# Decode attention over 640 instead of 1024 cached positions per sample in a hybrid decoder step

## The chip, the cores and the metric

The kernel runs on one core of one Trainium2 chip. The metric is the device time of one execution in microseconds. The core has TensorE (PE; its weight loads are listed as PEld), VectorE (DVE), ScalarE (ACT), GpSimd (POOL) and SyncE (SP), which issues most of the transfers; 16 DMA engines carry them.

## The reference

One inference step of one decoder layer: a prompt of 256 tokens and 8 samples of 4 new tokens (32 rows), 288 tokens together, all in fp32, with model width 1024. The normalized rows are projected by `w_in`, the attention and the state-space branch are joined and projected by `w_out`, and a mixture of 32 experts (top 4) follows. The part that the change touches is the attention of the samples, with 8 heads of 64 and a cache of 1024 past positions:

```python
DILATED_PATTERNS = ((128, 1), (512, 4), (2048, 16))

def dilated_attn_decode(q, k_all, v_all, slopes):
    T = q.shape[1]                      # 4
    M = k_all.shape[1] - T              # 1024
    for window, dil in DILATED_PATTERNS:
        steps = jnp.arange(window // dil + 1)
        idx = M + jnp.arange(T)[:, None] - dil * steps[None, :]
        valid = idx >= 0
        kg, vg = k_all[:, jnp.maximum(idx, 0)], v_all[:, jnp.maximum(idx, 0)]
        s = jnp.einsum('bthe,btkhe->bthk', q, kg) * scale
        bias = -slopes[:, None] * (dil * steps).astype(jnp.float32)[None, :]
        s = jnp.where(valid[:, None, :], s + bias, -jnp.inf)
        lse = jax.nn.logsumexp(s, axis=-1)
        outs.append(jnp.einsum('bthk,btkhe->bthe', jnp.exp(s - lse[..., None]), vg))
        lses.append(lse)
    return merge_by_denominator(outs, lses)
```

Past position p is reached by new token t if it lies within 128 of it, within 512 at a distance that is a multiple of 4, or at any distance that is a multiple of 16. So all positions from 512 on can be reached by one token or another (with t from 0 to 3, every residue of 4 occurs), and of the first 512 only those whose number is 0, 1, 2 or 3 modulo 16: 512 + 128 = 640.

## The kernel before

The kernel is one program with an order written out by hand for each engine. `mixer_steps()` returns the list `STEPS` that TensorE, VectorE and ScalarE all walk, each doing its own part of a step. The step `proj` is one of 32 projections of 128 output columns (8 matmuls of 288 columns each). Between the projections stand the steps of the samples' attention, of the prompt's attention (`p_score`, `p_trans`, `p_out`), of the convolution (`conv`, `silu`, `conv_out`), of dt (`dt`, `dt_sum`) and the turns of results back to token rows (`nat`).

The samples' attention computes all three patterns at once. Every position gets one bias, minus slope times distance plus the logarithm of the number of patterns that reach it, and -1e30 where none does; one softmax over all of them then gives the merged result. For each sample b there is a block of steps around two projections:
- `ktr`: VectorE turns the keys into columns, in four block transposes (32 by 32 blocks) of 128 by 1024 (L1231 to L1240), out of two ring slots into `kTb`, 16 times 288 columns: 256 columns of old positions (four positions side by side in the 128 lanes) and 32 new ones.
- `kscore`: TensorE makes 16 matmuls of 288 columns against the zero-padded queries `Qz` in four groups of 32 output partitions (L1827); VectorE adds the bias, keeps the maximum and writes `Pb` (L1263, L1264).
- `max_out`, `max_back`, `exp`, once for four samples: the maxima cross over TensorE (L1831, L1834), and ScalarE takes the exponentials (L904).
- `ptrans`: TensorE transposes the probabilities, two times 128 columns and once 32 (L1841, L1842), and ScalarE copies them back in another order (L909, L911).
- `pv`: 16 steps, 8 for each four samples; each is a tile of 128 positions of `cache_win_v` for four samples, 4 matmuls of 512 columns into bank 3 (L1859). `pv_new` adds the new rows (L1866), `gather_o` (L1870) puts the heads together.

Cached keys, cached values and `w_in` come through a ring of five 1 MB slots (`MIX_RING = 5`). `ring_items()` writes out the order: for each sample two halves of its keys and a pair of `w_in` tiles, then four times a pair of `w_in` tiles and four value tiles. SP issues them in this order (L574); the load of item n first waits until item n - 5 has been used (`mix_used`), and everything behind it in the queue waits too:

```python
            if kind == "w_in":
                eng.wait_ge(sem("w_used"), i // 2 + 1)
            elif kind == "k":
                eng.wait_ge(sem("k_used"), 2 * i + ITEMS[n][2] + 1)
            else:
                eng.wait_ge(sem("v_used"), i + 1)
```

After the mixer's steps come the scan of the states, the output projection (L2086), the router, and the experts (L2296, L2320), whose 192 weight units of 2 MB SP loads at L593. The last tile of `w_out` is loaded after a wait on `M_ready` (L577), and the first expert unit stands behind it in the queue.

Of the kernel before, what the change touches and what calls it, by code (L numbers as in the profile page):

```python
# [16 lines left out]
P = 128  # L17
# [7 lines left out]
PAST = 1024  # L25
# [43 lines left out]

XP = 3 + SEQ + DB * (3 + DT)  # L70
# [4 lines left out]
def shape_constants():  # L75
# [51 lines left out]
    put("bias_new", new.reshape(P, -1))  # L127
    consts = np.concatenate(parts, 1)
    col = np.arange(2 * P)
    d_old = PAST + t_row[:, None] - (2 * P * row_q[:, None] + 8 * (col % 32)[None, :] + (col // 32)[None, :])  # L130
    bias_old = bias(h_row[:, None], d_old).astype(np.float32)
# [8 lines left out]
def mixer_steps():  # L140
# [51 lines left out]
    steps.extend(("pv", t) for t in range(4))  # L192
# [6 lines left out]
    steps.extend(("pv", t) for t in range(4, 8))  # L199
# [9 lines left out]
    steps.extend(("pv", t) for t in range(8, 12))  # L209
# [7 lines left out]
    steps.extend(("pv", t) for t in range(12, 16))  # L217
# [33 lines left out]
ITEM_AT = {item: n for n, item in enumerate(ITEMS)}  # L251


def hymba_step(nc, a, o):

    ctx = ExitStack()
    with ctx:
# [34 lines left out]

        ident = const("ident")
# [51 lines left out]
        kTb = d3(work_take(16 * 288), 288)  # L345
# [4 lines left out]
        bias_o = work_take(2 * P)  # L350
        r_Pb = work_take(DB * 288)
        Pb = d3(r_Pb, 288)
# [21 lines left out]
        Xs = d3(const("bias_new"), P)  # L374
# [66 lines left out]
        def mix_used(eng, n):  # L441
# [4 lines left out]
            elif kind == "k":  # L446
                eng.wait_ge(sem("k_used"), 2 * i + ITEMS[n][2] + 1)
            else:
                eng.wait_ge(sem("v_used"), i + 1)
# [5 lines left out]
        def mix_full(eng, item):  # L455

            eng.wait_ge(sem(f"slot_full{mix_slot(item)}"), 16 * (ITEM_AT[item] // MIX_RING + 1))

        MIX_LOADS = [len([item for item in ITEMS if mix_slot(item) == s]) for s in range(RING)]
# [75 lines left out]
        def _(sp):  # L535
# [4 lines left out]
            w_out = a["w_out"][0].rearrange("(k p) c -> p k c", p=P)  # L540
            for n, item in enumerate(ITEMS):
# [7 lines left out]
                if item == ("v", 12):  # L549
# [17 lines left out]
                elif item[0] == "w_out":  # L567
                    dst, src = d3(slot(s), D), w_out[:, 2 * item[1]:2 * item[1] + 2, :]
                elif item[0] == "k":
                    dst, src = slot(s), a["cache_win_k"][0, item[1]].rearrange("(p k) h e -> p (k h e)", k=8)[:, SLOT * item[2]:SLOT * item[2] + SLOT]  # L570
                else:
                    grp, t = item[1] // 8, item[1] % 8
                    dst, src = d3(slot(s), AW), a["cache_win_v"][0, 4 * grp:4 * grp + 4, t * P:t * P + P].rearrange("b p h e -> p b (h e)")
# [197 lines left out]
        def _(act):  # L771
# [98 lines left out]
            for kind, i in STEPS:  # L870
# [34 lines left out]
                elif kind == "ptrans":  # L905
                    act.wait_ge(sem("ptrans_ps"), i + 1)
                    bank = 6 + i % 2
                    for half in range(2):
                        nc.scalar.activation(Pb[:, i, P * half:P * half + P].rearrange("p (q j c) -> p j q c", q=4, j=4),  # L909
                                             ps[:, bank, P * half:P * half + P].rearrange("p (j q c) -> p j q c", j=4, q=4), ACT.Copy)  # L910
                    nc.scalar.activation(d3(Pb[0:NS, i, 2 * P:2 * P + 32], 8), d3(ps[0:NS, bank, 2 * P:3 * P], 32)[:, :, 0:8], ACT.Copy).then_inc(sem("PT_ready"), 1)  # L911
# [212 lines left out]
        def _(dve):  # L1124
# [73 lines left out]
            for kind, i in STEPS:  # L1198
# [27 lines left out]
                elif kind == "krep":  # L1226
                    dve.wait_ge(sem("rep_ps"), 2)
                    nc.vector.tensor_copy(kTb[:, :, 2 * P:2 * P + NS].rearrange("p (j m) c -> p m j c", j=4),
                                          ps[:, 4, :].rearrange("p (m j c) -> p m j c", m=4, j=4)).then_inc(sem("krep_ready"), 1)
                elif kind == "ktr":  # L1230
# [3 lines left out]
                    for half in range(2):  # L1234
                        mix_full(dve, ("k", i, half))
                        rows = slot(mix_slot(("k", i, half))).rearrange("p (k m c) -> p k m c", k=4, m=16)
# [1194 lines left out]
```

## Time and profile before

| | us |
|---|---|
| median of 3 runs | 1264.44 (1264.29 to 1267.62) |
| span of the profiled execution | 1263.9 |
| TensorE busy | 1223.5 (97%) |
| VectorE busy | 373.5 (30%) |
| ScalarE busy | 241.7 (19%) |
| GpSimd busy | 49.2 (4%) |
| HBM read | 468.47 MB, 376 GB/s over the span |

An engine's busy time is the union of its instructions' times; TensorE's matmuls overlap, so that a busy TensorE need not be at its peak. An fp32 matmul is recorded as two instructions, and its duration includes its way through the array: the time that a row of them takes is read from the starts of its first and of the row that follows. In a timeline a line is a run of like instructions: start, length, engine, line of the kernel, operation, output and input, shape, count, and in brackets the idle time before it and what ended it. Of a shape like "128*32 128x288" the first part is rows by columns of the stationary operand, the second the moving one.

### The profile page before, as it was taken

How to read it: one execution, taken by the hardware profiler on the slowest of the kernel's cores; microseconds unless marked ns; L12 is line 12 of the kernel's file. 1: busy time of each engine (PE TensorE's matmuls, PEld its weight loads, DVE VectorE, ACT ScalarE, POOL GpSimd, SP SyncE). 2: the span in 40 equal slices, each digit the busy share in tenths (PEclk: the TensorE clock that was granted, in tenths of full speed). 3: DMA queues.
4: the chain of work that ended last, by engine and by line, in shares of the span. 5: the costliest groups of instructions: out<-in, count | busy, mean ns of one | idle time of the engine just before them, and what ended most of it. 6: DMA issues, size and time to landing. Idle time of an engine off the chain costs nothing.

```text
span 1263.9 us, 14652 instructions
## 1 busy us (share of the span) xinstructions
PE 1223.5 (97%) x5750; PEld 520.6 (41%) x5750; DVE 373.5 (30%) x756; ACT 241.7 (19%) x492; POOL 49.2 (4%) x46
## 2 busy tenths in 40 slices
PE   9999999999999999999999999999999999999997
PEld 6766666544433333333333333333333333333332
DVE  2468532775330321213031221213030312212122
ACT  2014343544201111120111111020111111111103
POOL 0000031503000000000000000000000000000000
PEclk9999999999999999999999999999999999999999
DMA  9697679249799999999999999999999999999996
GB/s 284 232 319 264 245 268 352 90 143 347 299 428 413 429 426 429 429 427 430 428 428 428 429 428 429 428 429 428 428 429 428 427 430 427 428 429 427 427 428 252
DMA packets 67439, 476.21 MB, mean 377 GB/s; under 512 B 7704, under 2 KB 25396, under 8 KB 40428
## 3 DMA queue, kind: packets, MB, share of 16 engines
q1 hardware_dynamic: 65278, 471.87, 91.0%
q10 hardware_dynamic: 1582, 2.03, 0.5%
q0 software_dynamic: 544, 1.84, 0.4%
q8 instruction: 23, 0.38, 0.1%
q14 instruction: 12, 0.10, 0.0%
HBM read 468.47 MB, written 7.24 MB: 376 GB/s over the span
## 4 chain that ended last, share of the span: by engine, by line
PE 75%; DMA 21%; DVE 2%; ACT 2%; issue 1%; SPq 0%; ACTq 0%; DVEq 0%
PE ps L2296 28%; DMA ring<-in_w 20%; PE ps L2320 11%; PE ps L1784 10%; PE ps L2234 4%; PE ps L2086 4%; PE ps L2226 2%; PE ps L2218 2%; PE ps L1827 1%; PE ps L2220 1%; PE ps L2284 1%; PE ps L2009 1%; PE ps L2304 1%; PE ps L1803 1%; PE ps L1859 1%
## 5 line engine op out<-in xcount | busy, mean ns | idle before, releaser
L2296 PE MATMUL ps<-ring,own 128*64 128x512 f32 x1536 | 340.1, 593 | 10.0 <-DMA ring<-in_w 10.0
L2296 PEld LDWEIGHTS ps<-ring,own 128*64 128x64 f32 x1536 | 111.7, 137 | 223.4 <-issue 194.3
L1658 DVE TENSOR_SCALAR own<-ps 128x512 f32<-128x512 f32 x32 | 22.1, 692 | 531.3 <-PE ps L2296 531.3
L2320 PE MATMUL ps<-ring,own 128*64 128x512 f32 x768 | 171.3, 594 | 4.7 <-ACT own L1055 4.6
L1784 PE MATMUL ps<-own,ring 128*128 128x288 f32 x512 | 131.6, 410 | 1.4 <-DVE own L1161 1.1
L2296 PE MATMUL ps<-own 128*64 128x512 f32 x512 | 115.9, 592 | 2.3 <-DMA own<-in_w 2.3
L1784 PEld LDWEIGHTS ps<-own,ring 128*128 128x128 f32 x512 | 95.7, 191 | 31.7 <-issue 3.3
L2320 PEld LDWEIGHTS ps<-ring,own 128*64 128x64 f32 x768 | 56.0, 137 | 111.3 <-issue 109.9
L2234 PE MATMUL ps<-own 128*128 128x512 f32 x180 | 88.5, 617 | 0.0
L1061 ACT ACTIVATE own<-ps 64x512 f32<-64x512 f32 x60 | 35.5, 592 | 206.5 <-PE ps L2320 205.8
L1649 DVE TENSOR_TENSOR own<-ps,own 128x512 f32<-128x512 f32 x34 | 21.9, 686 | 172.4 <-PE ps L2242 172.4
L2296 PEld LDWEIGHTS ps<-own 128*64 128x64 f32 x512 | 37.8, 136 | 68.3 <-issue 61.0
L2320 PE MATMUL ps<-own 128*64 128x512 f32 x256 | 58.5, 597 | 5.5 <-issue 4.1
L1050 ACT ACTIVATE own<-own 128x512 f32<-128x512 f32 x32 | 20.1, 627 | 217.2 <-DVE own L1658 217.2
L1055 ACT ACTIVATE own<-ps 128x512 f32<-128x512 f32 x32 | 19.1, 597 | 217.9 <-PE ps L2304 217.5
L2234 PEld LDWEIGHTS ps<-own 128*128 128x128 f32 x180 | 29.1, 187 | 48.5 <-issue 48.5
L2086 PE MATMUL ps<-ring,own 128*128 128x512 f32 x96 | 47.1, 612 | 0.0
L1239 DVE STREAM_TRANSPOSE ring<-ring 128x1024 f32<-128x1024 f32 x32 | 37.0, 1212 | 0.0
L2320 PEld LDWEIGHTS ps<-own 128*64 128x64 f32 x256 | 18.7, 135 | 39.3 <-issue 33.5
L2226 PE MATMUL ps<-own 128*128 128x512 f32 x64 | 31.8, 618 | 0.0
L2218 PE MATMUL ps<-own 128*128 128x512 f32 x64 | 31.8, 618 | 0.0
L2086 PEld LDWEIGHTS ps<-ring,own 128*128 128x128 f32 x96 | 16.3, 189 | 19.0 <-issue 18.8
(367 smaller groups left out, 978.3 us busy)
## 6 DMA issues: line engine op xcount, KB each, us to landing
ring<-in_w SPq DMA_DIRECT2D x143, 2048.0 KB, 29.7
own<-in_w SPq DMA_DIRECT2D x48, 2048.0 KB, 28.3
ring<-in_w_in SPq DMA_DIRECT2D x16, 1024.0 KB, 6.2
ring<-in_cache_win_k SPq DMA_DIRECT2D x16, 1024.0 KB, 6.6
ring<-in_cache_win_v SPq DMA_DIRECT2D x16, 1024.0 KB, 8.8
ring<-in_w_out SPq DMA_DIRECT2D x6, 1024.0 KB, 10.5
ring<-in_state_ssm SPq DMA_DIRECT2D x8, 512.0 KB, 10.3
out_ssm_sample<-ring SPq DMA_DIRECT2D x8, 512.0 KB, 9.6
```

The costliest lines, as they stand in the source:

```text
L1050: nc.scalar.activation(sg, xg, ACT.Sigmoid, scale=ALPHA).then_inc(sem("sig_ready"), 1)
L1061: nc.scalar.activation(ysb[C * u:C * u + C, 512 * half:512 * half + 512], ps[C * half:C * half + C, 4, :], ACT.Copy).then_inc(sem("ysb_rea ...
L1239: last = nc.vector.transpose(to[:, k:k + 2], rows[:, k:k + 2])
L1649: nc.vector.tensor_tensor(xT[:, 4 * half:4 * half + 4, :], d3(ps[:, 3 + 2 * half, :], 2 * C), vecs[:, 28 + 4 * half:32 + 4 * half].unsquee ...
L1658: nc.vector.tensor_scalar(xg_o, hid[:, 0], LIMIT, None, ALU.min).then_inc(sem("glu_ready"), 1)
L1784: last = nc.tensor.matmul(ps[:, i % 2, 0:TOK], w[:, k, (i % 2) * P:(i % 2) * P + P], xnT[:, k, :], start=(k == 0), stop=(k == KT - 1))
L2086: last = nc.tensor.matmul(ps[:, h_bank(c, half), :], mixT[:, k, cols(c)], w_rows(k)[:, 512 * half:512 * half + 512], start=(i == 0), stop= ...
L2218: nc.tensor.matmul(ps[:, 6 + half, :], GT[:, cols(0)], ysb[:, 512 * half:512 * half + 512], start=True, stop=True)
L2226: last = nc.tensor.matmul(ps[:, 3 + half, :], GT[:, cols(1)], ysb[:, 512 * half:512 * half + 512], start=True, stop=True)
L2234: last = nc.tensor.matmul(ps[:, 6 + half, :], S1[0:n, c, :], xn[0:n, c, 512 * half:512 * half + 512], start=(c == 0), stop=(c == 2))
L2296: last = nc.tensor.matmul(ps[C * half:C * half + C, 1 + m, :], xT[:, k, C * u:C * u + C], rows[:, D * half + 512 * m:D * half + 512 * m + ...
L2320: last = nc.tensor.matmul(ps[C * half:C * half + C, 4, :], gT[:, (k % 4) * P + C * (k // 4):(k % 4) * P + C * (k // 4) + C], rows[:, 512 * ...
```

## The change

Of each sample's 1024 old positions only 640 are loaded: the last 512 (from `LATE`) whole, and of the first 512 those whose number is 0 to 3 modulo 16, as 32 groups of 4 rows.
- Keys: one ring slot a sample instead of two (512 rows, two block transposes of 128 by 1024), and 128 early rows in one of two own buffers, `k_early`, with one transpose of 128 by 512. `kTb` and `Pb` have 192 columns instead of 288 (128 late, 32 early, 32 new). Before it loads the early rows of sample b (from 2 on), SP waits until both transposes of sample b - 2 are done.
- Values: 5 tiles instead of 8 for each four samples, the fifth made of early rows in four loads of 256 KB. The 10 `pv` steps stand where the 16 stood, 3, 2, 3 and 2 instead of 4 in each place, and the ring's order follows.
- `ptrans`: one full transpose, then for the 32 early columns four matmuls with picked columns of the identity, each into its own 32 partitions, then the transpose of the new columns. ScalarE copies 128, 32 and 32 columns instead of 128, 128 and 32.
- The bias of new rows and early rows comes with `bias_old` (640 columns, it was 256) and no longer with the constants (256 columns fewer). `Xs` gets its own place.

```diff
-            items += [("k", b, 0), ("k", b, 1), ("w_in", 8 + 2 * b)]
-    for i in range(4):
-        items += [("w_in", 24 + 2 * i)] + [("v", 4 * i + t) for t in range(4)]
+        items += [("k", b), ("w_in", 8 + 2 * b)]
+    for i, tiles in enumerate((range(3), range(3, 5), range(5, 8), range(8, 10))):
+        items += [("w_in", 24 + 2 * i)] + [("v", t) for t in tiles]
...
+            def early_rows(cache, sample):
+                return a[cache][0, sample, 0:LATE].rearrange("(g s) h e -> g s (h e)", s=STRIDE)[:, 0:DT]
...
-                if item == ("v", 12):
+                if item == ("v", 8):
                     sp.wait_ge(sem("conv_o"), 3)
...
+                elif is_early(item):
+                    for b in range(4):
+                        sp.dma_start(slot(s)[:, AW * b:AW * b + AW], early_rows("cache_win_v", 4 * (item[1] // TILES_V) + b)).then_inc(sem(f"slot_full{s}"), 16)
+                    continue
                 elif item[0] == "k":
-                    dst, src = slot(s), a["cache_win_k"][0, item[1]].rearrange("(p k) h e -> p (k h e)", k=8)[:, SLOT * item[2]:SLOT * item[2] + SLOT]
+                    b = item[1]
+                    if b >= 2:
+                        sp.wait_ge(sem("k_used"), 2 * b - 2)
+                    sp.dma_start(k_early[b % 2], early_rows("cache_win_k", b)).then_inc(sem(f"slot_full{s}"), 16)
+                    dst, src = slot(s), a["cache_win_k"][0, b, LATE:PAST].rearrange("(p k) h e -> p (k h e)", k=4)
...
+                    nc.vector.transpose(kTb[:, :, P:OLD], d3(k_early[i % 2], 32)).then_inc(sem("k_used"), 1)
...
-                            last = nc.tensor.matmul(ps[32 * j:32 * j + 32, 4 + i % 2, 0:288], Qz[:, 4 * j + m, i, :], kTb[:, 4 * j + m, :], start=(m == 0), stop=(m == 3))
+                            last = nc.tensor.matmul(ps[32 * j:32 * j + 32, 4 + i % 2, 0:OLD + NS], Qz[:, 4 * j + m, i, :], kTb[:, 4 * j + m, :], start=(m == 0), stop=(m == 3))
...
-                    for half in range(2):
-                        nc.tensor.transpose(ps[:, bank, P * half:P * half + P], Pb[:, i, P * half:P * half + P], ident)
-                    nc.tensor.transpose(ps[0:NS, bank, 2 * P:3 * P], Pb[:, i, 2 * P:2 * P + NS], ident).then_inc(sem("ptrans_ps"), 1)
+                    nc.tensor.transpose(ps[:, bank, 0:P], Pb[:, i, 0:P], ident)
+                    for q in range(4):
+                        own_rows = ident.rearrange("p (j q c) -> p q j c", j=4, q=4)[:, q]
+                        nc.tensor.matmul(ps[32 * q:32 * q + 32, bank, P:OLD], Pb[:, i, P:OLD], own_rows, start=True, stop=True)
+                    nc.tensor.transpose(ps[0:NS, bank, 2 * P:3 * P], Pb[:, i, OLD:OLD + NS], ident).then_inc(sem("ptrans_ps"), 1)
...
-                        w = d3(Pb[:, 4 * grp + b, P * (t % 2):P * (t % 2) + P], 32)[:, t // 2]
+                        w = d3(Pb[:, 4 * grp + b, 0:OLD], 32)[:, t]
```

## Rows read from the trace of the kernel before

**Rows 1.** Stretches: busy time of PE, PEld, DVE, ACT, POOL; clock, DMA share, GB/s
```profile
0.00:217.00 217.00, 210.26 (x1258) 144.54 (x1258) 105.42 (x274) 61.34 (x196) 18.00 (x23) 0.99 0.81 278
400.00:1200.00 800.00, 779.52 (x3396) 279.04 (x3394) 162.75 (x266) 105.12 (x167) 0.00 (x0) 1.00 1.01 428
```

**Rows 2.** The SP queue from 245 us: its longest wait; its timeline there
```profile
SPq L577 <- DVE own L1368: 48.4, 1, 48.4
...
265.71 0.42 SPq L593 DMA_DIRECT2D ring<-in_w  x1
```

**Rows 3.** TensorE's timeline around the scores of samples 1 and 2
```profile
69.51 2.15 PE L1827 MATMUL ps<-ring,own 128*32 128x288 f32 x32
71.58 4.16 PE L1784 MATMUL ps<-own,ring 128*128 128x288 f32 x16
...
80.22 2.15 PE L1827 MATMUL ps<-ring,own 128*32 128x288 f32 x32
```

**Rows 4.** TensorE's timeline around value tiles, and late in the stage
```profile
153.72 0.62 PE L1892 MATMUL ps<-own 128*59 128x128 f32 x4 [1.38 <-ACT ring L926]
...
166.34 3.62 PE L1859 MATMUL ps<-ring 128*32 128x512 f32 x32
169.89 0.78 PE L1884 MATMUL ps<-own 128*128 128x16 f32 x6
...
209.93 1.04 PE L1870 MATMUL ps<-ring,own 128*32 128x512 f32 x2
...
212.13 0.55 PE L1911 MATMUL ps<-own,ring 128*128 128x128 f32 x3
```

**Rows 5.** ScalarE's timeline from 161 to 167 us
```profile
161.38 0.40 ACT L930 ACTIVATE ring<-ring,own 128x128 f32<-128x128 f32 x1
...
161.78 0.49 ACT L931 ACTIVATE ring<-ring,own 128x256 f32<-128x256 f32 x1
...
166.53 0.41 ACT L915 ACTIVATE own<-ps 128x288 f32<-128x288 f32 x1 [0.71 <-PE ps L1878]
```

**Rows 6.** VectorE at sample 4 (key transposes, convolution, maxima); TensorE there
```profile
93.28 4.62 DVE L1239 STREAM_TRANSPOSE ring<-ring 128x1024 f32<-128x1024 f32 x4
...
101.97 0.27 DVE L1271 TENSOR_REDUCE own<-ps 4x32 f32<-4x128 f32 x1
...
92.36 4.16 PE L1784 MATMUL ps<-own,ring 128*128 128x288 f32 x16
...
102.55 0.22 PE L1834 MATMUL ps<-own 4*128 4x4 f32 x1 [1.36 <-DVE own L1272]
```

**Rows 7.** TensorE: transposes, the sum matmuls, four narrow records in one column group
```profile
108.78 0.49 PE L1803 MATMUL ps<-own 128*128 128x128 f32 x3
109.10 0.38 PE L1841 MATMUL ps<-own,ring 128*128 128x128 f32 x2
...
125.03 0.49 PE L1803 MATMUL ps<-own 128*128 128x128 f32 x3
125.45 0.24 PE L1846 MATMUL ps<-own 128*32 128x1 f32 x8
125.53 2.13 PE L1827 MATMUL ps<-ring,own 128*32 128x288 f32 x32
...
215.18 0.31 PE L1741 MATMUL ps<-own 128*32 128x32 f32 x4
215.42 0.23 PE L1748 MATMUL ps<-own 32*32 32x16 f32 x2
```

**Rows 8.** The wait of projection 30 on TensorE, and its load's issue on SP
```profile
190.69 4.16 PE L1784 MATMUL ps<-own,ring 128*128 128x288 f32 x16 [0.28 <-DMA ring<-in_w_in]
...
184.74 0.37 SPq L574 DMA_DIRECT2D ring<-in_w_in  x1
```

**Rows 9.** DMA issues from 60 to 138 us: count, size, median us to landing
```profile
ring<-in_cache_win_k SPq DMA_DIRECT2D x10, 1024.0 KB, 7.0
ring<-in_w_in SPq DMA_DIRECT2D x7, 1024.0 KB, 5.8
```

More of the change, by code:

```diff
@@ L126, in shape_constants @@
     new = np.where(own & (d_new >= 0), bias(h_row[:, None, None], d_new), NEG)
-    put("bias_new", new.reshape(P, -1))
     consts = np.concatenate(parts, 1)
-    col = np.arange(2 * P)
-    d_old = PAST + t_row[:, None] - (2 * P * row_q[:, None] + 8 * (col % 32)[None, :] + (col // 32)[None, :])
-    bias_old = bias(h_row[:, None], d_old).astype(np.float32)
+    col = np.arange(OLD)[None, :]
+    lane = 32 * row_q[:, None] + col % 32
+    place = np.where(col < P, LATE + 4 * lane + col // 32, STRIDE * (lane // 4) + lane % 4)
+    dropped = np.setdiff1d(np.arange(PAST), place)
+    assert place.size == np.unique(place).size * P // 4 and (bias(0, PAST + np.arange(DT)[:, None] - dropped) == NEG).all()
+    old = bias(h_row[:, None], PAST + t_row[:, None] - place)
+    tails = np.concatenate([np.broadcast_to(old[:, None, P:], new[:, :, 0:P // 4].shape), new], 2)
+    bias_old = np.concatenate([old[:, 0:P], tails.reshape(P, -1)], 1).astype(np.float32)
     d_prompt = r[:, None, None] + P - np.arange(2 * P)[None, None, :] + 0 * np.arange(AH)[None, :, None]
@@ L191, in mixer_steps @@
     steps.extend([("silu", 10), ("silu", 11), ("conv_out", 0)])
-    steps.extend(("pv", t) for t in range(4))
+    steps.extend(("pv", t) for t in range(3))
     steps.append(("conv_out", 1))
@@ L198, in mixer_steps @@
     steps.extend([("ptrans", 6), ("ptrans", 7), ("dt", 0), ("sums", 1)])
-    steps.extend(("pv", t) for t in range(4, 8))
+    steps.extend(("pv", t) for t in range(3, 5))
     steps.append(("dt_sum", 0))
@@ L208, in mixer_steps @@
     steps.extend([("p_out", 1), ("p_trans", 2), ("p_score", 3)])
-    steps.extend(("pv", t) for t in range(8, 12))
+    steps.extend(("pv", t) for t in range(5, 8))
     back(27)
@@ L216, in mixer_steps @@
     steps.extend([("p_out", 3), ("p_trans", 4), ("p_score", 5)])
-    steps.extend(("pv", t) for t in range(12, 16))
+    steps.extend(("pv", t) for t in range(8, 10))
     steps.append(("pv_new", 1))
@@ L455, in mix_full @@
         def mix_full(eng, item):
-            eng.wait_ge(sem(f"slot_full{mix_slot(item)}"), 16 * (ITEM_AT[item] // MIX_RING + 1))
-        MIX_LOADS = [len([item for item in ITEMS if mix_slot(item) == s]) for s in range(RING)]
+            before = [other for other in ITEMS[:ITEM_AT[item]] if mix_slot(other) == mix_slot(item)]
+            eng.wait_ge(sem(f"slot_full{mix_slot(item)}"), 16 * sum(loads_of(other) for other in before + [item]))
+        MIX_LOADS = [sum(loads_of(item) for item in ITEMS if mix_slot(item) == s) for s in range(RING)]
         def w_out_slot(i):
@@ L1865, in _ @@
                     for b in range(4):
[L1866 removed]
+                        last = nc.tensor.matmul(ps[32 * b:32 * b + 32, 3, :], Pb[0:NS, 4 * i + b, OLD:OLD + NS], v[0:NS, 2, :], start=False, stop=True)
                     last.then_inc(sem("pv_ps"), 1)
```

57 lines of the change are left out of this document (34 added, 23 removed).

## The prediction

> **What bounds the kernel now.** I read the table of stretches first [rows 1]. Up to 217 us (projections, attention, convolution) TensorE is busy for 210.3 us, and DMA has room (0.81 of its engines). Then the state scan and the output projection follow, to 340 us. From 400 us on the experts' weights arrive at 428 GB/s with the DMA share at 1.01. So the first stage is bound by TensorE's instructions in their written order, the last by the stream of weights. What is between them decides whether an early gain lasts: the queue of SP waits 48.4 us, in one piece, for VectorE's last decay product before it loads the last tile of w_out and, behind it, the first expert weights [rows 2]. Nothing of the stream is fetched ahead, so its start is tied to the end of the computation and moves one for one with it. I therefore add up what TensorE's path loses before 217 us and carry the sum to the end.
>
> An fp32 matmul stands in the trace as two records (the 32 projections of 8 matmuls are 512 records in the page), and columns count in it: the 16 score matmuls of one sample (32 records, 288 columns) take 2.07 us from their start to the start of the next work, the 16 value matmuls of four tiles (32 records, 512 columns) 3.55 us [rows 3, 4]. Per record that is 65 and 111 ns, ratio 1.71, against 1.78 in columns.
>
> **Scores.** Each sample's 16 matmuls go from 288 to 192 columns (128 + 32 old, 32 new). The two prices give (3.55 - 2.07) / 224 = 6.6 ns for each column of a set, with 0.17 us that stays. Then 96 columns fewer are 0.63 us, a set costs 1.44 us, and eight samples save **5.0 us**. All of it lies on the path: the next projection starts at the set's end [rows 3]. Bounds: 5.5 us if all of 2.07 us shrinks with the columns, nothing if the weight loads set the pace (a rival).
>
> **Values.** Ten tiles instead of sixteen, each 512 columns at 6.6 ns / 4 = 0.85 us to 3.55 / 4 = 0.89 us; at 0.87 six fewer are **5.2 us**. They go in four places (one, two, one, two tiles). In the last three the next waits are covered. After the second place the first thing needed is the evacuated dt product; ScalarE has it 0.60 us after the place where the tiles begin (166.94 against 166.34 us), and two tiles last 1.7 us [rows 4, 5]. After the third comes projection 30, whose weights I take below. After the last, a prompt score needs 2.2 us from its end to its transposes (209.93 to 212.13 us [rows 4]), against two tiles, 1.7, and the new rows' 1.0 us. In the first place it is not so. There TensorE already waits 1.38 us for ScalarE [rows 4], which first has to run four exponentials and two pairs of SiLU. Taking one tile away there lengthens the wait by 0.87 us. The exponentials shrink from 288 to 192 columns; the rows of 128 and 256 columns give 0.7 ns a column, 0.07 us each, 0.3 us for four [rows 5]. So **0.6 us** of the gain is given back.
>
> **VectorE's stall.** Each sample's keys cost four 32 by 32 block transposes of 1024 columns, 4.62 us; now two of 1024 and one of 512, 2.9 us (half of a long one, 0.6, for the short one; it is not in the trace, so 0.5 to 1.2). The biased copy of the scores shrinks too. From sample 3 on VectorE has 4.1 us of convolution behind them, and at sample 4 it is late: TensorE waits 1.36 us for the maxima [rows 6]. From the end of the previous scores (92.36 us) TensorE needs 8.8 us to the place of that wait (102.55 less 1.36). VectorE after the change needs 0.1 (start) + 0.6 (scores and maximum; 0.8 before, from 92.5 to 93.28 us) + 2.9 + 4.1 + 0.6 (maxima) = 8.3 us. The stall goes: **1.4 us** (1.1 if the short transpose costs as much as a long one). Next late is TensorE itself. The transposes of the other samples are covered, and their 14 us buy nothing.
>
> **Transposed probabilities.** Three transposes of a step take 0.32 us, 0.11 each (108.78 to 109.10 us [rows 7]). Of the three of a sample's probabilities one full one goes (0.11 us) and four matmuls of 32 columns come, each with its own 32 output partitions. The nearest rows are the four sum matmuls (weights 128 by 32, four column groups, one column): 0.08 us for 8 records. Before them the transposes of the step ahead, 0.32 us elsewhere, take 0.42 (125.03 to 125.45 us), so going over to narrow column groups costs 0.10 us; the 0.17 us left over in the score sets is the likely price of the way there and back [rows 3, 7]. Four small matmuls between two full transposes thus cost 0.08 + 0.05 for 31 more columns + 0.17 = 0.30 us, less 0.11: 0.19 us a sample, **+1.5 us** (bounds 0, if no switch is paid, and +4.5, if the records run one after the other at 60 ns as in one group, 215.18 to 215.42 us [rows 7]). I take 1.5 because it is made of rows with this very shape of weights. ScalarE's copies get no longer.
>
> The Trainium skill, "TensorEngine Tiling (Array Packing)", section "Instruction Overhead", says that a matmul has an overhead of about 60 cycles and that one with a free size of 1 takes as long as one of 60. Read as a floor for each record it would make the eight records 0.2 us instead of 0.13, an estimate from that page, and the sum 0.6 us smaller; the eight records in 0.08 us show groups side by side going below such a floor, and the sum keeps the row.
>
> **Transfers.** 12 of 32 MB of cached rows go. That buys little, since only 0.28 us of TensorE's idle time before 217 us is a wait for weights: projection 30, whose load was issued at 184.74 us because its slot was freed by projection 29 [rows 8]. In the new order of 5 slots that slot is freed by value tile 4, some 16 us earlier: **0.3 us**. The queue of SP issues as many loads as before (16 of keys; 8 of values and 8 quarters). New is its wait, from the third sample on, for the key transposes of two samples earlier. Behind it stand the keys of this sample and the next pair of w_in tiles, and TensorE and VectorE wait for those. The transposes end some 3.5 us after a sample's scores; the loads are wanted two periods after those, of 10.7 us now [rows 3] and 10.1 then, so some 16 us are there for landings of 7.0 and 5.8 us [rows 9]. Cost nothing while that cover lasts. The larger bias table (320 instead of 128 KB) lands long before the first scores near 60 us, the constants get 128 KB smaller, and neither touches a stall.
>
> **The sum:** 5.0 + 5.2 - 0.6 + 1.4 - 1.5 + 0.3 = 9.8 us. The profiled execution's span is 1263.9 us, 0.5 below the median of 1264.44, so it stands for the median, and 1264.4 - 9.8 = **1254.6 us**.
>
> **The rivals.**
> - *More of it (10%).* The narrow matmuls cost nothing, the scores shrink in proportion, and ScalarE gets ahead in the first place of value tiles too: 5.5 + 5.2 + 1.4 + 0.3 = 12.4, 1252.0 us. For it: 8 records in 0.08 us. Against: the 0.10 us seen ahead of them.
> - *Weight loads set the pace of the scores (6%).* The scores then save nothing: 4.8 us in all, 1259.6 us. For it: every one of the 16 matmuls has weights of its own to load. Against: the same loads pass at 10 ns a record in the sums, and pace follows columns [rows 3, 4, 7].
> - *The small pieces cost more (11%).* The narrow matmuls run one after the other (4.5 instead of 1.5 us), VectorE's short transposes cost as much as long ones and leave 0.3 us of the stall, and ScalarE lets one more value tile come to nothing (0.9): 9.8 - 3.0 - 0.3 - 0.9 = 5.6, 1258.8 us. For it: VectorE's thin reserve of 0.5 us, and the 60 ns a record in one column group.
> - *Slower (4%): the new wait starves the loads.* The early rows are 128 pieces of 2 KB, the quarters of a value tile four small transfers. If keys and w_in land more than 16 us after the freed buffer, samples 2 to 7 wait. From 1.6 us over that in each of the six it outweighs the gain; at 3 us over it is 18 - 9.8 = 8.2 us slower, 1272.6 us. Against: loads of 1 MB land after 6 to 9 us in this stage [rows 9], and DMA will be less busy. The Trainium skill, "DMA: Bandwidth & Descriptors", section "Bandwidth", speaks for this rival: it advises batches of at least 1 MiB. By that page's fixed cost of about 2 us, an estimate, a quarter would still be far inside the reserve.
>
> **How the numbers follow.** 69% for the forecast, whose own range is 1252.5 to 1257.5 us (terms off by up to 1.5 us for the narrow matmuls, 1 for the rest). The range that should hold 8 in 10 takes in the larger gain's near half and goes up toward the two weaker cases: 1251.5 to 1258.5 us. About 0.3% (3.8 us) is what a measurement of this kernel can tell from no change. Faster by more than that: 69 + 10 + 4 + 7 = 90%; within it, where the two weaker cases fall beyond their worked-out times: 6%; slower: 4%.
>
> **What would show it.** In the profile after: score sets at 1.44 us from start to start; value tiles at 0.87 us; key transposes at 2.9 us a sample; no idle time at the maxima of sample 4; an idle piece of about 2.0 us at the second conv_out; the four narrow matmuls of a transposition adding 0.3 us; the period of samples 1 and 2 at 10.1 us; projection 30 without a wait for DMA; and the first expert weights issued 9 to 10 us earlier (265.71 us before [rows 2]). I am wrong if the weights' issue does not move by what the first stage gained, if a score set stays near 2 us, or if a wait of TensorE for cache or w_in loads appears after 60 us.

## The result, and the profile after

The changed kernel takes 1256.91 us (median of 4 executions, 1254.69 to 1260.86), beside 1266.03 us (4 executions, 1264.29 to 1270.40) for the kernel before: a ratio of 0.992, 95% interval 0.990 to 0.9941. In a second comparison it was 1256.10 against 1267.24 us, 0.9908 (0.9884 to 0.9931). The time lies inside the range and 2.3 us above the forecast of 1254.6 us. The kernel is faster by more than 0.3%.

| profiled execution (us) | before | after |
|---|---|---|
| span | 1263.9 | 1258.6 |
| TensorE busy | 1223.5 | 1219.2 |
| VectorE busy | 373.5 | 359.5 |
| ScalarE busy | 241.7 | 241.2 |
| HBM read, MB | 468.47 | 455.95 |

The two spans differ by 5.3 us only, where 9.8 were forecast. To see why, the span is cut at three instructions that both kernels have: the first score set of sample 0, the first matmul of the state scan (L1952 before, L1992 after, the first `ps<-own 32*32 32x512`; the row of that shape at 199.81 us below also reads the ring and is the step `pv_new`), and the first expert matmul (the first `96*64 96x512`, L2284 and L2324).

| us | before | after | difference |
|---|---|---|---|
| start to first scores | 58.79 | 61.89 | +3.10 |
| first scores to scan ("the stage" from here on) | 161.36 | 151.40 | -9.96 |
| scan to first expert | 119.59 | 120.65 | +1.06 |
| first expert to end | 924.16 | 924.66 | +0.50 |

Every TensorE instruction that the change touches lies in the second row, and that row gained 9.96 us. In the first row TensorE's instructions are the same; changed there are the loads of the constants and of the first keys, and VectorE's transposes of sample 0's keys (three in 2.95 instead of four in 4.61 us, done before the first scores in both). The table of stretches shows what made the first row longer: columns are the stretch, its length, the busy time of PE, PEld, DVE, ACT and POOL, then the clock granted to TensorE, the DMA share and GB/s. After, from the start and around 324 us:

```profile
10.00:12.00 2.00, 2.00 (x9) 1.11 (x8) 0.67 (x4) 1.97 (x7) 0.00 (x0) 0.61 1.05 268
12.00:22.00 10.00, 8.93 (x28) 6.08 (x28) 4.30 (x11) 1.51 (x3) 0.00 (x0) 0.57 1.07 370
...
324.00:326.00 2.00, 2.00 (x11) 0.80 (x11) 0.36 (x2) 1.15 (x2) 0.00 (x0) 0.62 1.04 444
326.00:328.00 2.00, 2.00 (x5) 1.10 (x4) 1.24 (x7) 1.28 (x1) 0.00 (x0) 0.53 0.93 393
```

The same stretches of the kernel before, which stand at the lower level for a shorter time:

```profile
10.00:14.00 4.00, 3.00 (x18) 1.85 (x18) 1.92 (x9) 2.83 (x7) 0.00 (x0) 0.95 1.10 316
14.00:18.00 4.00, 3.89 (x10) 2.94 (x11) 2.96 (x7) 0.00 (x0) 0.00 (x0) 0.62 1.04 392
...
324.00:326.00 2.00, 2.00 (x9) 1.14 (x8) 0.69 (x1) 0.00 (x0) 0.00 (x0) 1.00 0.94 401
```

In this execution TensorE stood mostly at its lower level (0.5 of the full clock, 1.2 GHz) between 10 and 22 us; before it did so between 14 and 18 us. The other drop, at 324 to 328 us in the router, makes two matmuls last 1.93 and 1.89 us that take 1.12 and 1.10 us before. Whether these two drops come with the change or with the execution is left to the experiments; the stage holds neither. The weights' stream follows the stage's end, as the SP queue shows (longest wait, then its timeline), the answer to [rows 2]:

```profile
SPq L615 <- DVE own L1406: 48.6, 1, 48.6
...
258.78 0.42 SPq L631 DMA_DIRECT2D ring<-in_w  x1
```

The first expert weights are issued 6.93 us earlier than at 265.71 us, and 9.96 - 3.10 is 6.86. The 9 to 10 us earlier that the forecast named as a sign appear only when the late start is taken off: counted from the first scores, the issue comes 10.0 us earlier (196.89 instead of 206.92 us). The wait is as long as it was, 48.6 against 48.4 us: it moves as a whole.

TensorE after, in the places of [rows 3, 4, 6 and 7]: a score set; the place of the vanished wait for the maxima; the probabilities' transposes; the four places of value tiles.

```profile
71.97 1.51 PE L1865 MATMUL ps<-ring,own 128*32 128x192 f32 x32
73.41 4.16 PE L1822 MATMUL ps<-own,ring 128*128 128x288 f32 x16
...
101.24 0.49 PE L1841 MATMUL ps<-own 128*128 128x128 f32 x3
101.66 0.22 PE L1872 MATMUL ps<-own 4*128 4x4 f32 x1
...
107.58 0.27 PE L1878 MATMUL ps<-own,ring 128*128 128x128 f32 x1
107.78 0.27 PE L1881 MATMUL ps<-own,ring 128*32 128x32 f32 x8
107.98 0.28 PE L1882 MATMUL ps<-own,ring 128*32 128x128 f32 x1
108.10 0.27 PE L1878 MATMUL ps<-own,ring 128*128 128x128 f32 x1
...
146.03 2.78 PE L1899 MATMUL ps<-ring 128*32 128x512 f32 x24
150.73 0.62 PE L1932 MATMUL ps<-own 128*59 128x128 f32 x4 [1.92 <-ACT ring L964]
...
164.14 1.90 PE L1899 MATMUL ps<-ring 128*32 128x512 f32 x16
165.97 0.78 PE L1924 MATMUL ps<-own 128*128 128x16 f32 x6
...
182.85 2.78 PE L1899 MATMUL ps<-ring 128*32 128x512 f32 x24
185.56 4.16 PE L1822 MATMUL ps<-own,ring 128*128 128x288 f32 x16
...
197.96 1.92 PE L1899 MATMUL ps<-ring 128*32 128x512 f32 x16
199.81 1.06 PE L1906 MATMUL ps<-own,ring 32*32 32x512 f32 x8
```

The row of before ahead of the maxima's wait, which ends with the row at 102.55 us in [rows 6]:

```profile
100.69 0.49 PE L1803 MATMUL ps<-own 128*128 128x128 f32 x3
```

Read from start to start, a score set is 1.44 us (2.07 before); three value tiles are 2.71 us and two 1.83 and 1.85 (four were 3.55); projection 30, which follows at 185.56 us, no longer waits (0.28 us in [rows 8]). The row at 101.66 us has no bracket: the 1.36 us in front of the maxima are gone; from start to start the piece ahead of it takes 0.42 us (101.24 to 101.66) instead of 1.86 (100.69 to 102.55). The wait for ScalarE grew from 1.38 to 1.92 us. A sample's transposes last 0.52 us (107.58 to 108.10).

VectorE after, at sample 4, the answer to [rows 6]:

```profile
93.63 2.37 DVE L1276 STREAM_TRANSPOSE ring<-ring 128x1024 f32<-128x1024 f32 x2
95.92 0.67 DVE L1278 STREAM_TRANSPOSE ring<-ring 128x512 f32<-128x512 f32 x1
96.51 0.40 DVE L1284 TENSOR_SCALAR ring<-own 128x312 f32<-128x312 f32 x1
...
100.97 0.21 DVE L1310 COPY own<-own 4x128 f32<-4x128 f32 x1
```

The rows at 96.51 us and up to 100.97 us are convolution and the maxima. From 93.63 to 96.51 us is 2.88 us for a sample's keys. The copy of the maxima ends at 101.18 us, and TensorE would have come at some 101.56 (the row ahead of 101.66 lasts 0.32 us elsewhere): VectorE is 0.4 us early.

### The profile page after: what moved, and what is told of

Read it like the earlier page. It is cut to its first block, busy times and chain, and to the rows that moved or that the text cites. A ratio compares the mean times of both kernels' runs of the same rounds, so it can differ in the third digit from the quotient of the medians.

```text
span 1258.6 us, 14658 instructions
## 1 busy us (share of the span) xinstructions
PE 1219.2 (97%) x5758; PEld 521.2 (41%) x5758; DVE 359.5 (29%) x748; ACT 241.2 (19%) x492; POOL 49.2 (4%) x46
## 3 DMA queue, kind: packets, MB, share of 16 engines
HBM read 455.95 MB, written 7.24 MB: 368 GB/s over the span
## 4 chain that ended last, share of the span: by engine, by line
PE 76%; DMA 20%; ACT 2%; issue 1%; DVE 1%; SPq 0%; ACTq 0%; DVEq 0%
PE ps L2336 27%; DMA ring<-in_w 19%; PE ps L2360 12%; PE ps L1822 10%; PE ps L2274 5%; PE ps L2126 4%; PE ps L2266 2%; PE ps L2258 2%; PE ps L2260 1%; PE ps L2324 1%; PE ps L1865 1%; PE ps L2344 1%; PE ps L1841 1%; PE ps L2049 1%; PE ps L2166 1%
## 5 line engine op out<-in xcount | busy, mean ns | idle before, releaser
L2274 PEld LDWEIGHTS ps<-own 128*128 128x128 f32 x180 | 29.1, 187 | 48.5 <-issue 48.5
L2344 PEld LDWEIGHTS ps<-own 128*128 128x128 f32 x128 | 13.5, 141 | 25.6 <-issue 25.6
```

What stands on the lines that cost most here:

```text
L2274: last = nc.tensor.matmul(ps[:, 6 + half, :], S1[0:n, c, :], xn[0:n, c, 512 * half:512 * half + 512], start=(c == 0), stop=(c == 2))
L2344: last = nc.tensor.transpose(ps[:, 0, j * P:(j + 1) * P], gg[:, j * P:(j + 1) * P], ident)
```

## The experiments

All stages below run from the first score set to the scan, and each is read from one profiled execution of its kernel. Where a kernel was executed only once, the stage is the only measure, since a whole time carries the clock's scatter of several us.

**The changed kernel run anew.** Is the late start part of it?

```
(no edit)
```

> The changed kernel once more, on the same chip and against the same runs of before as the next. My sum says 9.8 us faster than before, ratio 0.992; the stage 151.4 us again; the rest of the span differs only by how long the clock is low. If what was measured first was partly luck of the clock, the ratio moves by more than 0.002.

Measured: 1256.10 us (6 executions, 1253.83 to 1259.55) against 1267.24 us (11 of before, 1263.82 to 1272.45). The profiled execution again has its first scores late (61.68 us), the stage is again 151.40 us, and from the scan to the first expert it takes 120.65 us again. But both profiles are of executions with a mean clock of 0.994 (1260.86 and 1259.55 us), the slowest of their groups; the same kernel also ran at 0.999 and 1.000, in 1254.69 and 1253.83 us, where 12 us at half the clock have no room. And six variants of it, below, whose TensorE instructions up to the first scores are the same, have those at 57.28 to 60.28 us. Over all twelve profiles of this document the start goes with the time at the lower level between 8 and 24 us, worked out from the granted clock of stretches of 2 us: first scores at 57.23 and 57.28 us where there is none, at 58.76 to 59.24 us in seven profiles with 3 to 4 us of it (the kernel before is one), at 60.28 us with about 7, at 61.68 and 61.89 us with about 10. The late start belongs to the clock of the execution, not to the kernel. The mean clock of an execution orders the times of both kernels: before, five executions at 1.000 lie at 1263.60 to 1264.78 us, four at 0.998 at 1266.26 to 1267.24, two at 0.992 at 1272.45 and 1272.62; after, 1253.83 at 1.000, 1256.03 and 1256.18 at 0.998, 1259.55 at 0.994, where four of before lie at 1270.09 to 1270.38. Each of the ten executions of the changed kernel, set against the mean of before at the same rounded clock, is 9.3 to 10.9 us faster, 10.3 in the mean.

**The scores alone**, in the kernel before.

```diff
-    ... ps[32 * j:32 * j + 32, 4 + i % 2, 0:288], Qz[...], kTb[:, 4 * j + m, :] ...
+    ... ps[32 * j:32 * j + 32, 4 + i % 2, 96:288], Qz[...], kTb[:, 4 * j + m, 96:288] ...
```

> The kernel before, in which the 16 score matmuls of each sample stream 192 columns (96 to 288) instead of 288; the first 96 columns of scores are left out, all else is as it was. Stage length, from the start of the first score set to the start of the first matmul of the state scan (L1952): 161.4 us before, 151.4 after the change. My sum: a set falls from 2.07 to 1.44 us, the stage to 156.4 us (up to 156.9, since VectorE is now nearly as long as TensorE in samples 3 to 7), the stall of 1.36 us at sample 4 stays; whole kernel 4.5 to 5 us faster. Rival, weight loads set the pace of the scores: a set stays at 2.0 us and the stage at 161 us.

Measured: 0.9967 (0.995 to 0.9984; 1262.31 against 1267.77 us). The stage is 158.21 us: 3.15 us less, not 5.0. The score sets did what was forecast (first two rows); a lower clock and a new wait took part of it back (the others). TensorE's timeline of this kernel:

```profile
58.95 1.51 PE L1827 MATMUL ps<-ring,own 128*32 128x192 f32 x32
60.39 4.16 PE L1784 MATMUL ps<-own,ring 128*128 128x288 f32 x16
...
88.53 1.51 PE L1827 MATMUL ps<-ring,own 128*32 128x192 f32 x32
90.73 1.97 PE L1784 MATMUL ps<-own,ring 128*128 128x288 f32 x7 [0.69 <-DMA ring<-in_w_in]
...
100.42 0.22 PE L1834 MATMUL ps<-own 4*128 4x4 f32 x1 [0.87 <-DVE own L1272]
...
168.70 5.66 PE L1784 MATMUL ps<-own,ring 128*128 128x288 f32 x16
174.29 1.05 PE L1870 MATMUL ps<-ring,own 128*32 128x512 f32 x2
```

and its stretches around the last of them:

```profile
164.00:168.60 4.60, 4.60 (x36) 2.12 (x29) 1.81 (x10) 1.52 (x2) 0.00 (x0) 0.99 1.06 393
168.60:170.00 1.40, 1.40 (x5) 1.11 (x4) 0.94 (x4) 1.37 (x4) 0.00 (x0) 0.50 1.06 388
170.00:172.00 2.00, 2.00 (x5) 1.35 (x5) 1.90 (x9) 0.54 (x1) 1.28 (x1) 0.52 1.05 386
```

A set is 1.44 us, so eight save 5.04. The projection at 168.70 us takes 5.59 us from start to start instead of 3.99: the clock fell to 1.2 GHz for 3.4 us behind 4.60 us in which TensorE was busy throughout, and that cost 1.6 us. And a wait of 0.69 us for `w_in` is new; the wait for the maxima behind it is 0.87 us, so that the two together are 1.56 us where 1.36 stood. 161.36 - 5.04 + 1.60 + 0.20 = 158.12, and 158.21 was measured. The drop falls into the stage in the profiled execution; against executions of before at the same rounded mean clock the ten of this kernel are 4.6 to 6.2 us faster, 5.1 in the mean, which is near the 4.8 us that are left without it. The rival in which weight loads set the pace of the scores falls.

**The bytes alone**, in the kernel before: 10.5 of the 12 MB less.

```diff
-                    dst, src = slot(s), a["cache_win_k"][...][:, SLOT * item[2]:SLOT * item[2] + SLOT]
+                    n_k = SLOT if item[2] == 0 else AW
+                    dst, src = slot(s)[:, 0:n_k], a["cache_win_k"][...][:, SLOT * item[2]:SLOT * item[2] + n_k]
...
-                    ... a["cache_win_v"][0, 4 * grp:4 * grp + 4, t * P:t * P + P] ...
+                    n_v = 1 if t in (2, 5, 7) else 4
+                    ... a["cache_win_v"][0, 4 * grp:4 * grp + n_v, t * P:t * P + P] ...
```

> The kernel before, with 10.5 MB fewer of cached rows loaded: the second half of each sample's keys is a quarter of its size, and so are 6 of the 16 value tiles (what isn't loaded keeps the slot's old contents); all computation is as it was. My sum: the stage keeps 161.4 us (at most 0.3 less, the wait of projection 30), and the whole kernel is the same within 0.5 us. Rival, the smaller traffic itself is a good part of the gain (fewer bytes in SBUF and HBM, loads landing earlier): the stage comes to 156 us or less.

Measured: 1.001 (0.9989 to 1.003), the stage 161.24 us, 0.12 less. The waits for ScalarE and for the maxima are as long as before (1.4 us each), and of the 0.3 us for `w_in` 0.2 are left. By themselves the bytes bring nothing: this third of the cache traffic hides behind TensorE's work.

**Scores and bytes together**, the two edits above in one kernel.

> The kernel before, with both earlier edits: score matmuls of 192 columns (the first 96 columns of scores left out) and 10.5 MB fewer of cached rows. With the scores alone TensorE waited 0.69 us for w_in at sample 4. If that wait came from the traffic, it is gone here, VectorE's stall is back at 1.36 us and the stage is 156.0 us; if it came from the order in which slots are freed, it stays, and the stage is 156.2 us with the stall at 0.9. Both leave out any drop of the clock.

Measured: the stage is 156.55 us. No wait for `w_in` stands at sample 4 any more, the wait for the maxima is 1.6 us, and no drop of the clock falls into the stage: 161.36 - 5.04 + (1.6 - 1.36) = 156.56.

```profile
98.70 0.23 PE L1836 MATMUL ps<-own 4*128 4x4 f32 x1 [1.63 <-DVE own L1274]
```

That is 0.55 us above the forecast: the stall came back 0.27 us longer than the 1.36 us, and the wait of 0.3 us at projection 30 is still there, where 161.36 - 5.04 less that wait would be the 156.0 of the forecast. The wait of 0.69 us in the kernel with the scores alone thus came from the traffic. It cost nothing there, since VectorE was late behind it anyway. In the changed kernel, where VectorE is no longer late, it would have cost up to 0.69 us; that is worked out, and no run shows it.

**Value tiles in the first place**: the third and fourth `pv` step done twice in the changed kernel, one of them in the first place, one in the second.

```diff
+                    if i in (2, 3):
+                        for b in range(4):
+                            w = d3(Pb[:, 4 * grp + b, 0:OLD], 32)[:, t]
+                            last = nc.tensor.matmul(ps[32 * b:32 * b + 32, 3, :], w, vc[:, b, :], start=False, stop=False)
```

> The changed kernel, with the four matmuls of the third value tile and those of the fourth done twice (a sum that is then wrong): one tile more in the first place, where TensorE waits 1.92 us for ScalarE, one more in the second. My sum: the first costs nothing (the wait falls to 1.05 us), the second its 0.87 us; stage 151.4 + 0.9 = 152.3 us. Rival, each tile is on the path: 153.1 us.

Measured: the stage is 152.26 us, 0.86 more. In the first place the extra tile shortens the wait for ScalarE and moves nothing:

```profile
141.41 2.78 PE L1899 MATMUL ps<-ring 128*32 128x512 f32 x24
144.01 1.04 PE L1903 MATMUL ps<-ring 128*32 128x512 f32 x8
146.12 0.62 PE L1936 MATMUL ps<-own 128*59 128x128 f32 x4 [1.06 <-ACT ring L964]
```

From 141.41 to 146.12 us is 4.71 us with four tiles, and 4.70 (146.03 to 150.73) with three. In the second place nothing takes the tile's 0.87 us back: the stage grew by 0.86 us. ScalarE does set the first place.

**VectorE's transposes**: one more transpose of 128 by 1024 for each sample, into unused space, in the changed kernel.

```diff
+                    scratch = sub(r_xbcT, 8 * TOK, SLOT // 2)
+                    last = nc.vector.transpose(scratch.rearrange("p (k m c) -> p k m c", k=2, m=16), rows[:, 2:4])
```

> The changed kernel, with one more 128x1024 block transpose on VectorE for each sample (into unused space), so 4.0 us of key transposes instead of 2.9; 9.1 us more work for VectorE in all. My sum: the reserve at the maxima of sample 4 is about 0.4 us, so a stall of 0.7 to 0.8 us comes there and nothing elsewhere: stage 152.2 us. Rival, VectorE is as long as TensorE in samples 3 to 7 and each added transpose counts there: 5 x 1.1 more, 157 us.

Measured: the stage is 152.12 us, 0.72 more, for eight transposes of 1.12 us each (from start to start; the one at sample 4 begins at 93.27 us and the next row at 94.39). The list of TensorE's waits has one new row:

```profile
PE ps L1874 <- DVE own L1312: 0.6, 1, 0.6
```

The stall is back at sample 4 and there alone, and 1.12 less the reserve of 0.4 us is 0.7. The transposes of the other samples are covered, with and without the change.

**SP's new wait with one period less of reserve**, in the changed kernel.

```diff
-                        sp.wait_ge(sem("k_used"), 2 * b - 2)
+                        sp.wait_ge(sem("k_used"), 2 * b)
```

> The changed kernel, with SP's new wait made one sample stricter: the keys of sample b, and the w_in tiles behind them, are issued only when the keys of sample b - 1 are turned (it was b - 2). In the profile after, 16 us lay between; now some 6 us, against landings of 5.6 us for keys and 7.6 us for w_in. My theory of the reserve: TensorE waits for w_in by 0.5 to 2 us a sample, the stage gets 4 to 14 us longer (155 to 165 us, against 151.4). Rival, the wait has room in any case: 151.4 us.

Measured: the stage is 165.08 us, 13.7 more. The loads then wait for the keys of the sample just before. TensorE's timeline, and its waits up to 230 us:

```profile
72.83 5.74 PE L1822 MATMUL ps<-own,ring 128*128 128x288 f32 x16 [2.29 <-DMA ring<-in_w_in]
78.41 0.49 PE L1841 MATMUL ps<-own,ring 128*128 128x128 f32 x3
...
98.53 6.53 PE L1822 MATMUL ps<-own,ring 128*128 128x288 f32 x16 [4.55 <-DMA ring<-in_w_in]
104.90 0.49 PE L1841 MATMUL ps<-own 128*128 128x128 f32 x3
...
PE ps L1822 <- DMA ring<-in_w_in: 9.4, 4, 4.6
```

9.4 us are waits for `w_in`, in four places (4.6, 2.3, 1.3 and 1.3 us), where 0.5 to 2 us in each sample were expected; the projections behind the two long ones take 5.58 and 6.37 us instead of 4.00, and the granted clock stood at 0.50 to 0.66 from 72 to 76 us and from 96 to 104 us: 4.0 us more. The two make 13.4 of 13.7 us. The mechanism of the slower rival is real, and in the changed kernel it is one period away. There SP does stand at its new wait, 42.4 us in five waits between 57 and 215 us, but that costs nothing: sample 3's keys and its `w_in` tiles are issued at 66.89 to 68.11 us, and TensorE begins the projection that reads those tiles at 83.49 us. No wait of TensorE or VectorE for a cache or `w_in` load is left in the stage.

**The narrow matmuls done twice**, in the changed kernel.

```diff
-                    for q in range(4):
+                    for q in 2 * tuple(range(4)):
```

> The changed kernel, with the four narrow matmuls of each sample's early columns done twice in a row (same result). The trace after shows 0.52 us for a sample's three pieces instead of 0.33. My price is 0.08 + 0.05 us for the records and 0.17 us for the way into narrow column groups and back: the second set adds only 0.13 us a sample, the stage 1.0 us, 152.4 us. By a floor of 25 ns for each record (the Trainium skill, TensorEngine Tiling, Instruction Overhead, read so) it adds 0.2 us and the stage is 153.0; at 60 ns a record, one after the other, 155.2 us.

Measured: the stage is 151.90 us, 0.50 more, half of what the forecast's price of 0.13 us for eight records would give. The row of the records, and what follows:

```profile
106.16 0.33 PE L1881 MATMUL ps<-own,ring 128*32 128x32 f32 x16
106.43 0.28 PE L1882 MATMUL ps<-own,ring 128*32 128x128 f32 x1
```

Sixteen records take 0.27 us, eight took 0.20 (107.78 to 107.98): 0.07 us for eight more, 8 ns a record with 32 columns each (0.50 us in eight samples is 0.06 for eight records).

The Trainium skill ("TensorEngine Tiling (Array Packing)", section "Instruction Overhead") gives each matmul about 60 cycles, and by that, an estimate from that page, eight records would take 0.2 us more. The 0.07 us measured here do not bear that out for records in column groups side by side.

**A plain transpose in their place.** It turns the 32 early columns into one block of 32 partitions, and so what the value matmuls read of the early positions is not their probabilities.

```diff
-                    for q in range(4):
-                        own_rows = ident.rearrange("p (j q c) -> p q j c", j=4, q=4)[:, q]
-                        nc.tensor.matmul(ps[32 * q:32 * q + 32, bank, P:OLD], Pb[:, i, P:OLD], own_rows, start=True, stop=True)
+                    nc.tensor.transpose(ps[0:P // 4, bank, P:2 * P], Pb[:, i, P:OLD], ident)
```

> The changed kernel, with the four narrow matmuls replaced by one transpose of the 32 early columns into 32 partitions (the probabilities of the early positions are then wrong). My price: 0.52 us of a sample's transposes become 0.33, the stage loses 1.5 us, 149.9 us. If the narrow matmuls cost nothing (the larger-gain rival), 151.4 us.

Measured: the stage is 151.51 us and contains a drop of the clock (0.62 at 164 to 166 us, 0.53 at 166 to 168). The projection that begins there takes 5.48 us instead of 3.99, and the transposes ahead of it 0.57 instead of 0.39; with these 1.67 us taken off it is 149.84 us, where 149.9 was expected. TensorE's timeline:

```profile
104.44 0.27 PE L1878 MATMUL ps<-own,ring 128*128 128x128 f32 x1
104.55 0.27 PE L1879 MATMUL ps<-own,ring 128*32 128x128 f32 x1
104.66 0.27 PE L1880 MATMUL ps<-own,ring 128*32 128x128 f32 x1
104.77 0.27 PE L1878 MATMUL ps<-own,ring 128*128 128x128 f32 x1
```

Three pieces take 0.33 us (104.44 to 104.77), against 0.52 with the four narrow ones: 0.19 us a sample, 1.5 in eight, and 151.40 - 149.84 = 1.56. With the run before it this splits the price. Four narrow matmuls cost 0.30 us (0.52 less two pieces at 0.11). 0.07 of it is what eight more records cost. The other 0.23 us are paid once, however many records follow: 0.09 us ahead of them (107.58 to 107.78 is 0.20 instead of 0.11), the rest within their own row. The price does not come from stationary operands of 32 columns as such: L1879 and L1880 have those, in the first column group alone, and take 0.11 us each. That it is the way to the other column groups and back fits this, but no run tells it from another fixed cost of the first narrow matmuls.

The Trainium skill says on the same page, in section "Key Properties", that a change of the tiling mode drains TensorE; it names no price. The 0.23 us would agree with such a drain on the way there and back, but no run here shows one.

**Another order**, an attempt to use what was learned: the matmuls that wait for ScalarE move back, behind a projection or a value place, and the wait of 0.7 us for the turn of one projection goes by splitting a pair of them. Same work, other order.

```diff
-    back(21, 2)
+    back(21)
...
     proj(25)
+    back(21)
...
-    steps.extend([("silu", 10), ("silu", 11), ("conv_out", 0)])
+    steps.extend([("silu", 10), ("silu", 11)])
     steps.extend(("pv", t) for t in range(3))
-    steps.append(("conv_out", 1))
+    steps.append(("conv_out", 0))
     proj(26)
-    steps.extend([("ptrans", 4), ("ptrans", 5), ("conv_out", 2), ("p_score", 0)])
+    steps.extend([("conv_out", 1), ("ptrans", 4), ("ptrans", 5), ("conv_out", 2), ("p_score", 0)])
```

> The changed kernel with its steps in another order around projections 24 to 26: one nat step of a pair goes behind projection 25, the value tiles come before the first conv_out, and projection 26 before the second. It computes the same. My theory, ScalarE's chain of exponentials and SiLU takes back the gain of the first place: TensorE's waits of 1.92 and 0.71 us go, the stage is 148.8 to 149.2 us, and the kernel 2.2 to 2.6 us faster than after_again. Rival, ScalarE is simply late and the wait reappears at projection 26 or the second conv_out: 151 us.

Measured: the stage is 148.39 us, 3.0 less than in the changed kernel; 1253.92 us (6 executions, 1252.57 to 1254.80) against 1256.10 of the changed kernel on the same chip, and 0.9892 (0.9869 to 0.9915) of the kernel before. TensorE in the first place:

```profile
141.69 2.78 PE L1900 MATMUL ps<-ring 128*32 128x512 f32 x24
144.41 0.65 PE L1933 MATMUL ps<-own 128*59 128x128 f32 x4
...
148.79 0.60 PE L1933 MATMUL ps<-own 128*59 128x128 f32 x4
```

Neither of the two convolution outputs has a wait in brackets. The 1.92 us and the 0.7 us are gone, 2.6 of the 3.0; the rest is spread over the starts of the moved rows, none of it over 0.13 us. What the change gave back to ScalarE, and the 1.38 us that were there before it, were a matter of order. The medians differ by 2.2 us only, but at equal rounded clock the difference is about 3: at 0.998 three executions at 1252.57 to 1253.88 us stand against 1256.03 and 1256.18 us, at 0.996 1253.96 against 1257.32 us. The missing 0.8 us go with the clock.

## Why the prediction was right

The terms of the sum in us, each as measured in the one profile of each kernel (minus is a gain):

| term | forecast | measured | from |
|---|---|---|---|
| scores | -5.0 | -5.04 | 0.63 us in each of eight sets; the same with the scores alone |
| values, less what ScalarE takes back | -5.2 + 0.6 | -4.71 | places 0.33, 1.72, 0.93, 1.73 |
| VectorE's stall | -1.4 | -1.44 | 1.86 to 0.42 us in front of the maxima |
| transposed probabilities | +1.5 | +1.5 | 0.19 us a sample |
| projection 30 | -0.3 | -0.28 | wait gone |
| sum | -9.8 | -9.97 | the stage: -9.96 |

The places before were 148.69 to 153.72, 166.34 to 169.89, 186.77 to 190.41 and 203.08 to 206.66 us.

- **The bound.** That TensorE's written order bounds the stage, and that its end drags the stream of weights along, held: the scan to the first expert took 119.56 to 119.67 us in six of the ten experiments, whatever the stage had cost (148.39 to 165.08 us). The other four took 120.64 to 121.11 us, and in each of them the clock is down for 3 to 4 us in the router (0.50 to 0.57 at 324 us, 322 us, 330 us and 336 us).
- **Scores.** The forecast of 1.44 us a set, from the price per column and the fixed part, held to 0.01 us.
- **Values.** The first place took 4.70 instead of 5.03 us: of one tile's 0.87 us, 0.54 were given back to ScalarE (forecast: 0.6), and the extra tile there cost nothing.
- **VectorE.** Transposes of 2.88 us (2.9), a reserve of 0.4 us (0.5), and behind it, as forecast, TensorE itself. The added transposes show that the other samples' 14 us were cover.
- **Narrow matmuls.** The total of 0.30 us was right, its split was not. The step that failed is "0.08 + 0.05 for 31 more columns + 0.17": eight records add 0.07 us and not 0.13, and the part paid once, which the forecast called the way there and back, is 0.23 and not 0.17. Two errors of 0.06 us with opposite signs cancelled, which was luck. For a kernel with more narrow matmuls behind one switch, the forecast's prices would have been wrong.
- **Transfers.** "That buys little" holds for the bytes alone (0.12 us). The step left out that a quicker TensorE asks for its weights earlier: with the old traffic and the new scores a wait of 0.69 us for `w_in` appeared. The smaller traffic is what keeps it away, and the sum had this right only because it took both at once. That was luck too: the forecast does not name this effect.
- **SP's new wait.** The forecast reserve of some 16 us was right: 66.89 to 83.49 us is 16.6. Taking one period away cost 13.7 us; the forecast priced an overrun by the wait alone and left out that the clock falls with it, 4.0 us of those 13.7. Its reading that loads of 1 MB land after 6 to 9 us in this stage was narrow: before, the value loads issued from 138 us on took 10.1 us in the median, still inside the reserve.
- **The level.** 1254.6 us rested on a median of three executions of before that lay low, 1264.44; larger groups of the same kernel gave 1267.77 (19) and 1267.24 us (11). Working from the profile's own span did not help, since its clock too was nearly full. Of the 2.3 us by which 1256.91 lies above the forecast, 1.6 are this level (before took 1266.03 us beside it); the other 0.7 are the difference between a gain of 9.8 and one of 9.1 us, less than the scatter of the clock. At equal clock the gain is 10.3 us, as above; at a mean clock of 1.000 the changed kernel took 1253.83 us. The closeness of 1256.91 to 1254.6 us thus says less than the stage does: 9.96 us against 9.8. The 1.06 us between scan and experts are a drop of the clock in the router, as above, and not a term that the sum lacks. The 0.50 us in the experts have no cause that I found; the experiments lie on both sides of it (923.49 to 925.95 us).

## What to carry to other kernels

Where one engine's written order bounds a stage, price each edit by the time from the start of its first row to the start of the next work, and ask at every place which other engine TensorE waits for next: in one place of four, that wait took more than half of a tile's gain, and a new order of the steps got it back. A transfer that is hidden now need not be hidden for an engine made quicker; judge less traffic together with the edit that makes the stage shorter. Measure a stage between two instructions that both kernels have before comparing whole spans, since a few us of lower clock elsewhere can be as large as the effect.

## What the hardware showed beside that

- TensorE's granted clock fell to its lower level, 1.2 GHz, for 3 to 4 us in the middle of the kernel in some executions although TensorE was busy throughout ahead of it: at 168.6 us with the scores alone, at 164 and 322 us with the plain transpose, at 324 us in both profiles of the changed kernel. Each cost 1 to 1.7 us. Two more drops of that length, at 330 us with scores and bytes together and at 336 us with the bytes alone, came behind stretches in which TensorE had gaps (busy for 3.07 of 4 and 1.22 of 2 us), and the two in the kernel with the later SP wait came with waits of 2.29 and 4.55 us. At the start the lower level lasted from 10 to 22 us in both profiles of the changed kernel, 3 to 4 us in the kernel before, and did not appear at all with the extra value tiles or with scores and bytes together (1.00 throughout 8 to 24 us). What decides where it falls stays open.
- The mean clock of an execution tells its time within about 1 us: before, 1.000 goes with some 1264, 0.998 with 1266 to 1267, 0.996 with 1267 to 1269, 0.994 with 1270, 0.992 with 1272.5 us.
- Loads of 256 KB in pieces of 2 KB landed 3.1 us after their issue, those of 1 MB of keys after 5.6 and of `w_in` after 7.6 us, beside one another (median, 60 to 138 us of the changed kernel): small pieces had no penalty that reached TensorE.
